# Down projection of an MLP on one Trainium2 core: three of four quarters token-major with seven block products, weight sums on GpSimd

## The reference

```python
u = rms_norm(h, norm_mlp_g[l])
h = h + jnp.square(jax.nn.relu(u @ w_mlp1[l])) @ w_mlp2[l]
```

## Time and profile before

| what | us |
| --- | --- |
| median of 3 runs | 1350.39 |
| lowest and highest run | 1349.81, 1351.56 |
| span of the profiled execution, first to last instruction | 1348.7 |
| median less that span, what lies around it | 1.7 |
| TensorE busy in that span | 1334.4 |
| VectorE, ScalarE, GpSimd busy | 939.1, 586.7, 70.7 |

### The profile page before, as it was taken

The page is one execution under the profiler, slowest core; times in us unless marked ns, Lnnn a source line. Parts: engine busy times, 40 slices in busy tenths (PEclk is TensorE's granted clock), DMA queues, the critical chain, the costliest instruction groups (busy, mean ns, idle before and its releaser), DMA issues.

```text
span 1348.7 us, 17627 instructions
## 1 busy us (share of the span) xinstructions
PE 1334.4 (99%) x6397; PEld 1094.9 (81%) x6397; DVE 939.1 (70%) x1503; ACT 586.7 (43%) x990; POOL 70.7 (5%) x60
## 2 busy tenths in 40 slices
PE   7999999999999999999999999999999999999998
PEld 6787777788888888888888888888888888888886
DVE  7868888885576543355445563599889988995685
ACT  7535655564555432114333344734333433333234
POOL 1000000102002000000013300000000000000000
PEclk9999999999999999999999999999999999999999
DMA  5333333243323333323333342323233223323332
GB/s 164 94 93 79 73 74 89 63 141 97 107 80 107 95 93 110 93 76 112 94 93 93 94 121 83 97 78 93 73 98 95 82 76 89 87 74 109 98 106 94
DMA packets 224104, 127.02 MB, mean 94 GB/s; under 512 B 21234, under 2 KB 214851, under 8 KB 224034
## 3 DMA queue, kind: packets, MB, share of 16 engines
q1 hardware_dynamic: 222418, 123.47, 31.9%
q10 hardware_dynamic: 1616, 2.62, 0.6%
HBM read 123.98 MB, written 2.10 MB: 93 GB/s over the span
## 4 chain that ended last, share of the span: by engine, by line
PE 97%; DVE 2%; ACT 1%; issue 0%; ACTq 0%; DVEq 0%
PE lin L668 26%; PE lin L671 26%; PE lin L672 26%; PE ob L1095 1%; PE sc L760 1%; PE sc L1051 1%; PE sc L1054 1%; PE sc L1055 1%; PE tr L773 1%; PE ob L797 1%; PE sc L784 1%; PE tr L1054 1%; PE lin L1054 1%; PE tr L1055 1%; PE lin L1055 1%; PE tr L1051 1%
## 5 line engine op out<-in xcount | busy, mean ns | idle before, releaser
L1719 DVE TENSOR_TENSOR wl<-raw,wh 128x1024 fp32r<-128x1024 f32 (+2 forms) x235 | 287.2, 1230 | 62.1 <-ACT wh L1228 57.7
L1228 ACT ACTIVATE wh<-raw 128x1024 fp32r<-128x1024 f32 (+2 forms) x235 | 238.8, 1022 | 134.9 <-DMA raw<-in_w_mlp_dram 44.2
L668 PE MATMUL lin<-uh,wh 128*128 128x512 f32 x624 | 249.8, 400 | 0.5 <-DVE ul L1791 0.4
L672 PE MATMUL lin<-uh,wl 128*128 128x512 f32 x624 | 243.2, 390 | 0.0
L671 PE MATMUL lin<-ul,wh 128*128 128x512 f32 x624 | 243.1, 390 | 0.0
L668 PE MATMUL lin<-vh,wh 128*128 128x512 f32 x512 | 202.6, 396 | 0.2 <-DVE te L2369 0.2
L671 PE MATMUL lin<-vl,wh 128*128 128x512 f32 x512 | 199.6, 390 | 0.0
L672 PE MATMUL lin<-vh,wl 128*128 128x512 f32 x512 | 199.3, 389 | 0.0
L668 PEld LDWEIGHTS lin<-uh,wh 128*128 128x128 f32 x624 | 117.2, 188 | 27.8 <-issue 4.4
L671 PEld LDWEIGHTS lin<-ul,wh 128*128 128x128 f32 x624 | 117.3, 188 | 25.1 <-issue 2.2
L672 PEld LDWEIGHTS lin<-uh,wl 128*128 128x128 f32 x624 | 117.1, 188 | 24.7
(11 more groups left out here) (555 smaller groups left out, 2085.2 us busy)
## 6 DMA issues: line engine op xcount, KB each, us to landing
raw<-in_w_in_dram SPq DMA_DIRECT2D x100, 512.0 KB, 3.8
raw<-in_w_mlp_dram SPq DMA_DIRECT2D x64, 512.0 KB, 4.0
raw<-in_w_out_dram SPq DMA_DIRECT2D x16, 512.0 KB, 3.7
raw<-in_w_xkv_dram SPq DMA_DIRECT2D x8, 512.0 KB, 3.7
raw<-in_w_proj_b_dram SPq DMA_DIRECT2D x8, 512.0 KB, 3.8
raw<-in_w_proj_a_dram SPq DMA_DIRECT2D x8, 512.0 KB, 3.7
xtok<-in_x_dram ACTq DMA_DIRECT2D x4, 512.0 KB, 5.0
raw<-in_w_mla_out_dram SPq DMA_DIRECT2D x4, 512.0 KB, 3.5
```

The lines of the kernel that those rows point to most:

```text
L668: ins = pe.matmul(o, wh[:, slot, at], xh_, start=start, stop=False)
L672: return pe.matmul(o, wl[:, slot, at], xh_, start=False, stop=stop)
L1228: act.activation(wh[:, c.slot(4), 0:size], raw[:, c.slot(2), 0:size], ACT.Copy).then_inc(hi_made, 1)
L1719: dve.tensor_tensor(wl[:, c.slot(4), 0:size], raw[:, c.slot(2), 0:size], wh[:, c.slot(4), 0:size].bitcast(F32), ALU.subtract).then_inc(lo_ ...
```

## The change

**Quarters.** The hidden features are taken in four quarters of 1024. `up` of a quarter: 8 jobs as before. `down` of quarters 0 to 2 is token-major, with seven block products; `down3` is feature-major as before, 8 jobs of one chunk each.

**Seven products.** The tokens are two halves of 256, the output features two halves of 512, and the hidden tiles of a quarter are paired, even and odd (four pairs kk). VectorE makes four sums of activation blocks per pair (`sums`, 128 x 256 each), ScalarE their high parts, VectorE their low parts (`sums_low`). GpSimd makes sums of weight blocks: three dependent ones per pair while chunks 0 to 7 pass, and one per pair later, 16 adds of 128 x 512 per quarter. A quarter has 14 chunks of 12 matmuls: chunks 2kk and 2kk+1 carry four products of a pair into the banks X, Q, P and R, chunks 8 to 13 carry three. Each product is 2 token blocks x 3 parts per pair.

**Loads.** A quarter has 12 loads through three raw slots (`raw2` is new): for r under 8 the whole even tile (512 KB) and the right half of the odd tile (256 KB) in turns, then the four odd tiles whole. Load r waits for the slot of r - 3, that is for the low part of that chunk, and for some of them a sum.

**Sums of products.** VectorE adds the banks into 14 blocks of 128 x 512 in SBUF (`part`; copies in quarter 0). In `up3` it combines them in 16 adds (`combine`), TensorE turns them back to feature-major with 32 transposes in the middle of jobs (`turn_acc`), and VectorE scales them and adds them to `h` (`turned_added`).

**Order.** The loops of the MLP are written out. The norm's reciprocal is waited for inside `up0`. The bias table of VectorE stands in `down3` after job 4, GpSimd's iota and mask behind the quarters. Some semaphores between two VectorE instructions are replaced by the common `step`. `acc` of the convolution is renamed `cacc`.

The core of the diff (leading blanks cut):

```diff
@@ -66,8 +66,8 @@
 PHASES = [("latent", 6, 6), ("conv", 8, 8), ("mvalues", 1, 0), ("heads", 28, 28), ("mla_out", 4, 8), ("conv_out", 4, 8),
-  ("w_out", 12, 12), ("xq", 4, 4), ("xv", 4, 0), ("xo", 4, 8), ("up0", 16, 16), ("down0", 16, 8), ("up1", 16, 16),
-  ("down1", 16, 8), ("values", 8, 0), ("av", 8, 0),
+  ("w_out", 12, 12), ("xq", 4, 4), ("xv", 4, 0), ("xo", 4, 8), ("up0", 8, 8), ("down0", 14, 0), ("up1", 8, 8),
+  ("down1", 14, 0), ("up2", 8, 8), ("down2", 14, 0), ("up3", 8, 8), ("down3", 8, 8), ("values", 8, 0), ("av", 8, 0),
...
+sh = sb("sh", [P, 4, 2, 256], F32R)
+sl = sb("sl", [P, 4, 2, 256], F32R)
+acc = sb("acc", [P, 4, 2, S])
...
+s4h = sb("s4h", [P, 4, 256], F32R, st)
+s4l = sb("s4l", [P, 4, 256], F32R, st)
+acc5 = sb("acc5", [P, 2, S], stack=st)
+raw2 = sb("raw2", [P, 1024], stack=st)
...
+RAW_SLOTS = (raw[:, 1, :], raw[:, 0, :], raw2[:])
+SLOT_LANDED = (raw_landed[1], raw_landed[0], raw2_landed)
+T2S = (vtok[:].rearrange("p q d -> p (q d)"), logit[:, 512:1024], qt[:], kt[:])
+SF = first_turned[:].rearrange("p t x -> p (t x)")[:, 0:1024].rearrange("p (n t) -> p n t", n=4)
+PART_X, PART_Q, PART_P, PART_R = (sc[0], sc[1]), (lin[0], lin[1]), (sc[2], ob), (tr[0], tr[1])
+atok_flat = atok[:].rearrange("p q d -> p (q d)")
+SUM_X1, SUM_P, SUM_X2, SUM_R2 = ((acc[:, n, 0, :], acc[:, n, 1, :]) for n in range(4))
+SUM_Q1, SUM_Q2, SUM_R1 = (acc5[:, 0, :], acc5[:, 1, :]), (nlog[:], bias[:]), (atok_flat, te[:])
+ACC_BLOCKS = ((SUM_X1, SUM_R2), (SUM_Q2, SUM_Q1))
...
+    def seven_free(u, r):
+        c = SEVEN0[u]
+        if r < 8:
+            sp.wait_ge(lo_made, c + r + 1)
+            if r == 6:
+                sp.wait_ge(sums_made, seven_sum(u, 3, 3))
+        else:
+            sp.wait_ge(lo_made, c + r + 1 + (r > 9))
+            sp.wait_ge(sums_made, seven_sum(u, r - 8, 4))
+    for q in range(4):
+        c, _ = phase(f"up{q}")
+        for m in range(DT):
+            if q and m < 2:
+                seven_free(q - 1, 9 + m)
+            load(c + m, a["w_mlp1"][0], q * FFQ + P * m, DT, P)
+        c, _ = phase(f"down{q}")
+        rows = a["w_mlp2"][0][q * FFQ:(q + 1) * FFQ, :]
+        if q == SEVENS:
+            for m in range(DT):
+                load(c + m, rows, P * m, DT, P)
+            continue
+        for r in range(SEVEN_LOADS):
+            if r < 2:
+                sp.wait_ge(lo_made, c.static - 1 + r)
+            elif r == 2:
+                if q:
+                    seven_free(q - 1, 11)
+                else:
+                    sp.wait_ge(lo_made, c.static)
+            else:
+                seven_free(q, r - 3)
+            kk, odd = (r // 2, r % 2) if r < 8 else (r - 8, 1)
+            first, n = (512, 512) if r < 8 and odd else (0, 1024)
+            tile = 2 * kk + odd
+            sp.dma_start(RAW_SLOTS[r % 3][:, 0:n], rows[tile * P:(tile + 1) * P, first:first + n])\
+                .then_inc(SLOT_LANDED[r % 3], 16)
...
+    add_squares("mlp")
+    for u in range(SEVENS):
+        first = SEVEN0[u]
+        for kk in range(4):
+            ra, rb = 2 * kk, 2 * kk + 1
+            even, odd = RAW_SLOTS[ra % 3], RAW_SLOTS[rb % 3]
+            pool.wait_ge(SLOT_LANDED[ra % 3], seven_landed(u, ra))
+            pool.wait_ge(SLOT_LANDED[rb % 3], seven_landed(u, rb))
+            if kk:
+                pool.wait_ge(sums_made, seven_sum(u, kk - 1, 3))
+            pool.tensor_tensor(odd[:, 512:1024], even[:, 512:1024], odd[:, 0:512], ALU.add).then_inc(sums_made, 1)
+            pool.wait_ge(sums_made, seven_sum(u, kk, 1))
+            pool.tensor_tensor(even[:, 512:1024], even[:, 0:512], even[:, 512:1024], ALU.add).then_inc(sums_made, 1)
+            pool.wait_ge(sums_made, seven_sum(u, kk, 2))
+            pool.tensor_tensor(T2S[kk], even[:, 512:1024], odd[:, 0:512], ALU.add).then_inc(sums_made, 1)
+        for kk in range(4):
+            r = 8 + kk
+            pool.wait_ge(SLOT_LANDED[r % 3], seven_landed(u, r))
+            pool.wait_ge(lo_made, first + 2 * kk + 2)
+            pool.tensor_tensor(T2S[kk], T2S[kk], RAW_SLOTS[r % 3][:, 0:512], ALU.add).then_inc(sums_made, 1)
+    pool.wait_ge(std_made, NORM_NO["mlp"] + 1)
+    pool.wait_ge(lo_made, CHUNK0["up3"])
+    pool.memset(sum_h[:], 0.0).then_inc(sums_cleared, 1)
+    pool.memset(sum_x1[:], 0.0).then_inc(sums_cleared, 1)
+    pool.wait_ge(sums_cleared, 2)
+    pool.wait_ge(h_added, DT)
...
+    def seven_part(banks, left, k, weights, slot, half, first, last, signal):
+        at = slice(512 * half, 512 * half + 512)
+        high, low_ = left
+        for r in range(2):
+            tok = slice(k + r * P, k + (r + 1) * P)
+            ins = pe.matmul(banks[r][:], high[:, tok], wh[:, slot, at], start=first, stop=False)
+            if weights and r == 0:
+                ins.then_inc(chunk_entered, 1)
+            pe.matmul(banks[r][:], low_[:, tok], wh[:, slot, at], start=False, stop=False)
+            ins = pe.matmul(banks[r][:], high[:, tok], wl[:, slot, at], start=False, stop=last)
+            if signal:
+                ins.then_inc(part_ready, 1)
...
+    def seven(u):
+        c, j = phase(f"down{u}")
+        for kk in range(4):
+            even, odd = (fh[:, 2 * kk, :], fl[:, 2 * kk, :]), (fh[:, 2 * kk + 1, :], fl[:, 2 * kk + 1, :])
+            s2, s3 = ((sh[:, kk, n, :], sl[:, kk, n, :]) for n in range(2))
+            last = kk == 3
+            x, y = c + 2 * kk, c + (2 * kk + 1)
+            pe.wait_ge(f_low, 12 * u + 3 * kk + 3)
+            pe.wait_ge(lo_made, (x + 1).v())
+            if kk == 0:
+                if u:
+                    taken(u - 1, 10)
+            seven_part(PART_X, even, 0, True, x.slot(4), 0, kk == 0, last, last)
+            if kk == 0:
+                evacuated(pe, j + -2)
+                evacuated(pe, j + -1)
+            seven_part(PART_Q, even, 256, False, x.slot(4), 1, kk == 0, last, last)
+            pe.wait_ge(lo_made, (y + 1).v())
+            seven_part(PART_P, s2, 0, True, y.slot(4), 0, kk == 0, last, last)
+            if kk == 0:
+                if u:
+                    taken(u - 1, 14)
+                else:
+                    pe.wait_ge(std_made, NORM_NO["mlp"] + 1)
+            seven_part(PART_R, s3, 0, False, y.slot(4), 1, kk == 0, last, last)
+        for g in range(2):
+            for kk in (2 * g, 2 * g + 1):
+                odd, s4 = (fh[:, 2 * kk + 1, :], fl[:, 2 * kk + 1, :]), (s4h[:, kk, :], s4l[:, kk, :])
+                w = c + (8 + kk + g)
+                pe.wait_ge(lo_made, (w + 1).v())
+                if kk == 0:
+                    taken(u, 2)
+                seven_part(PART_X, odd, 0, True, w.slot(4), 0, kk == 0, kk == 3, kk == 3)
+                if kk == 0:
+                    taken(u, 4)
+                seven_part(PART_Q, s4, 0, False, w.slot(4), 1, kk == 0, kk == 3, kk == 3)
+            w = c + (10 + 3 * g)
+            pe.wait_ge(lo_made, (w + 1).v())
+            if g == 0:
+                taken(u, 8)
+            for n in range(2):
+                kk = 2 * g + n
+                odd = fh[:, 2 * kk + 1, :], fl[:, 2 * kk + 1, :]
+                seven_part(PART_R, odd, 256, n == 0, w.slot(4), n, kk == 0, kk == 3, kk == 3)
...
+    def turn_acc(f):
+        if f > 1:
+            pe.wait_ge(h_added, f - 1)
+        for q in range(QT):
+            block = ACC_BLOCKS[f // 4][q // 2]
+            ins = pe.transpose(tr[f % 2][:, q * P:(q + 1) * P], block[q % 2][:, (f % 4) * P:(f % 4 + 1) * P],
+                               ident[:])
+        ins.then_inc(part_ready, 1)
+    for q in range(4):
+        c, j = phase(f"up{q}")
+        for m in range(DT):
+            if q and m < 2:
+                taken(q - 1, 11 + m)
+            if q == SEVENS and m in (1, 5):
+                taken(SEVENS - 1, SEVEN_PARTS + (8 if m == 1 else 16))
+            job(c + m, j + m, DT, uh, ul, before=tiles_of(u_low, U0["mlp"]) if q == 0 and m == 0 else None,
+                between={4: lambda f=m - 1: turn_acc(f)} if q == SEVENS and m else {})
+            if q == 0 and m == 3:
+                sum_total("mlp")
+        if q < SEVENS:
+            seven(q)
+    c, j = phase("down3")
+    for m in range(DT):
+        job(c + m, j + m, DT, fh, fl, before=tiles_of(f_low, 12 * SEVENS) if m == 0 else None,
+            between={4: lambda: turn_acc(DT - 1)} if m == 0 else {})
...
+    def seven_split(c):
+        u = sum(c.static >= first for first in SEVEN0) - 1
+        v, slot = c.static - SEVEN0[u], c.slot(4)
+        kk = v // 2
+        if v < 8 and v % 2 == 0:
+            act.wait_ge(sums_made, seven_sum(u, kk, 2))
+            wait(act, chunk_entered, (c + -2).v())
+            act.activation(wh[:, slot, :], RAW_SLOTS[v % 3], ACT.Copy).then_inc(hi_made, 1)
+        elif v < 8:
+            act.wait_ge(sums_made, seven_sum(u, kk, 3))
+            wait(act, chunk_entered, (c + -2).v())
+            act.activation(wh[:, slot, 0:512], T2S[kk], ACT.Copy)
```

(109 more changed lines are left out.)

227 lines of the change are left out of this document (91 added, 136 removed).

## The result

The changed kernel takes 1394.15 us (median of 4 runs, 1393.18 to 1395.21), beside 1350.39 us before (also of 4 runs): 1.0325 times as long, with a 95% interval of 1.031 to 1.0339. Forecast were 1392 us, 1371 to 1410, slower with 0.91. The profiled execution has a span of 1393.5 us. Its own time was 1395.2 us, the longest of the four.

What follows compares the result with a forecast made beforehand. The prediction took TensorE to bound the kernel, with chunk preparation too slow after the change. Its terms, -16.3 + 4.5 + 44.8 + 3 + 6 = +42, added to the median of 1350.4 gave 1392 us, range 1371 to 1410.

Steps and rivals of the forecast that it cites:

- 72 products less: Down quarters 0 to 2: 168 products each instead of 192, at 0.227 us, saving 16.3 us on the path.
- 32 transposes: Added on TensorE: 128 x 128 transposes at 0.14 us each, 4.5 us, taken whole.
- waits of three quarters: Down quarters 0 to 2: TensorE waits 14.9 us per quarter for prepared chunks, 44.8 in all, bounds 32 to 58.
- combining in up3: In up3 TensorE's second job waits for VectorE to add up the accumulators: 3 us, 2 to 4.
- bias table in down3: In down3 the table's twelve VectorE steps after job 4 delay freeing job 5's bank: 6 us, 1 to 9.
- up0: First up phase: the forecast sum has no term for it.
- The ring: First four chunk pairs of a down quarter: closed chain load, two adds, high part, low part, 8.2 us against 5.44 of work.
- The port: VectorE and GpSimd in down quarters: an add and a VectorE operation wait for each other, some 1.1 us per add.
- rival 1: Down quarters: port costs little because VectorE and GpSimd happen to miss each other; +31, 1381 us; chance 0.18.
- The quarter's 14.9: Waits in each of down quarters 0 to 2, before Q banks and chunks 1, 2, 4, 6 and 8: 14.9 us together.
- The rival on the other side: Down quarters: TensorE stays the bound and keeps the whole gain, 1338.6 us; chance 0.07.

Runs made afterwards that it cites:

- turned_no_sums: Changed kernel with extra landing slot, reordered queues at the up-to-down turn, bias table and waits moved, GpSimd's weight sums left out: 1341.7 us.
- no_sums: Changed kernel without GpSimd's 48 weight adds and all waits for them: 1363.5 us.
- four_slots: Changed kernel with a fourth raw landing slot, so a load may run a chunk earlier: 1388.1 us.
- fills: Changed kernel with each GpSimd weight add replaced by three write-only fills of nearly the same total length, all waits kept: 1383.1 us.
- three_edits: Changed kernel with the bias table moved to the av phase, up3's wait put right before its transposes, X banks taken before chunk 9's low part: 1382.3 us.
- turned_early: Changed kernel with extra slot, moved table and waits, reordered turn, plus chunks 0 to 2 earlier and 3 and 4 before the last up job's sums: 1371.7 us.

## Why the prediction was right

By its own steps, measured in the changed kernel:

| step | predicted | measured |
|---|---|---|
| 72 products less | -16.3 | -15.8 (43.5 to 38.3 in each of three quarters, turned_no_sums) |
| 32 transposes | +4.5 | +3.8 (0.12 each in up3, 0.5 in down3) |
| waits of three quarters | +44.8 (32 to 58) | +44.0 (14.8, 15.2, 14.0), of it 31.6 waits |
| combining in up3 | +3 (2 to 4) | +2.7 |
| bias table in down3 | +6 (1 to 9) | +9.2 |
| up0 | 0 | +0.9 |
| sum | +42 | +44.8 by spans, +43.8 by medians |

The rows for the quarters and for down3 compare lengths of phases, so they hold slow products too; what that hides stands below.

**The ring.** Predicted 8.2 us per pair, measured 7.8. It is the chain that was written down: from the end of chunk 2's low part (571.98) to the first add 2.7 (load and issue were put at 2.9), two adds to 577.29 with 2.6, high part and hops 1.1, low part 1.3. The load of 256 KB landed in 2.6 us, estimated at 2.7. That it is this chain, not VectorE or TensorE, is shown by no_sums and four_slots, which each take the waits before chunks 4 and 6 away.

**The port.** Predicted 1.1 us per add that meets a VectorE operation; the row shows 1.78 for 0.69, the same 1.1. The fills show that reading is what hurts: same waits, nearly the same duration, no slowing. The Trainium skill's rule (SBUF — State Buffer, Who interferes with whom), that a VectorE instruction with two SBUF inputs and a GpSimd read exclude each other for a whole instruction, agrees with these rows; rival 1 needed luck, and didn't get it.

**Where the total hides errors.** The quarter's 14.9 was right as a sum, but not in its parts. Predicted were 2.6 (Q banks and chunk 1), 4.8 (chunk 2), 2.7 and 2.7 (chunks 4 and 6), 2.0 (chunk 8). Down1 has 1.4, 4.4, 0, 2.3 and 2.6, 3.9 us of slow products and 0.6 in small pieces. Of the slow products, 2.3 us stand between chunk 2's gap and chunk 4: they fill the time in which TensorE would have waited for chunk 4, whose low part ends at 579.75, 2.2 us after a chunk 4 at full speed would have been due (572.12 + 5.44). So that wait would have been about what was predicted. The 1.6 us behind chunk 8's gap have no later wait to hide them and are a plain loss.

Over the three quarters the 44.0 us are 31.6 of waits (10.7, 10.7, 10.2), 10.4 of products at half speed and 2.0 in small pieces. By the same reckoning, an estimate, 8.4 of the 10.4 (2.9, 2.3 and 3.1) stand in front of a further wait and only took its place, so at full speed the waits would have been about 40 us, not 44.8. The mechanism was right, the ring above all. That the total fits to 2 us is in part luck: the start of a quarter cost less than predicted, and half speed, which was not in the sum, made up for it.

**What was mis-sized.** The bias table: 9.2 where 6 was taken, with 9 as the bound. The 6 was a choice between its bounds, not a sum. Of the 9.2, 7.2 go with the table's place (three_edits); 1.6 of the 9.2 are products at half speed behind the gap of 6.8. The other 2 stay without the table. What the sum left out shows in the rows: VectorE's round of a job was taken as its free length, but its low part takes 2.34 us in place of 1.22 with one of GpSimd's square sums inside. Its rounds are 6.5 us long (783.59 to 790.12) where TensorE's are 5.44, so VectorE falls back by 1.1 us per job and the table starts late. No run took those square sums away, so their share isn't measured by itself. A wait of 0.9 us before down0's first product stood in the sum at nothing.

**The rival on the other side** (1338.6 us, TensorE stays the bound) needed waits under 3.9 us per quarter. turned_no_sums shows that its arithmetic was right, 1341.7 with 2 us of down3 left, and that only the sums stand between: it would need adds that neither lie in the chain nor take VectorE's port.

So of the 44 us, by runs: 11 to 14 are the port (fills; 11 by the medians, 14 by the quarters), 17 to 20 the adds' time in the chain (fills to no_sums), 22 the order of the queues, the slots, the table and the combining (no_sums to turned_no_sums), 3 are left in turned_no_sums, and against them stand the 12 that products less transposes give back. The shares overlap: with a better order, taking the sums away gives 21 us instead of 31.

## What to carry to other kernels

When a change lets each loaded block feed fewer products, compute the preparation as a closed ring (load, add, high part, low part, slot free) and hold it against the new time per block, before counting the products saved: here 7.8 against 5.44 us foretold the slower kernel. It isn't the only limit, though: with the ring opened (four_slots) only 6 us came back, since the same adds then met VectorE's work at the turn. An idle engine isn't a free one: GpSimd was busy 5% of the time before, and the 62 us of adds given to it cost VectorE up to 36 us, most of it in operations with two SBUF inputs at the turn from up to down. And a saving of 16 us spread over three phases is gone with one wait of 5 us in each.

## What was not expected of the hardware

**Half speed behind a gap.** After TensorE had waited 4.27 us, the granted clock in the changed kernel was 0.50 (third column from the end of this window's row), and products started 0.43 us apart:

```profile
572.10:574.70 2.60, 2.58 (x6) 2.12 (x7) 1.08 (x2) 0.00 (x0) 0.04 (x1) 0.50 0.47 137
```

That is 1.2 GHz in place of 2.4. Eleven products ran so there, 2.3 us lost. It isn't the same each time: behind chunk 6's gap of 2.25 in down1 no product was slow, behind the one of 2.26 in down2 eight were, from the sixth on (1.6 us); behind the gaps of 1.75 us in down1 and down2 of no_sums none was, behind the 2.77 in its down0 eight were, and in turned_no_sums, without gaps, none in the quarters. So a long wait cost up to about 3 us on top of its length in these kernels (2.96 in down1 of turned_early, behind 4.96), unless the next wait hides it. A stretch's granted clock shows it at once.

**Small operations suffer most.** VectorE's sums of 256 columns take 0.42 us alone and 1.37 to 1.51 beside GpSimd's adds, over three times as long, where 1024 columns take 1.9 for 1.22: the surcharge is 0.7 to 1.1 us per operation, whatever its size. That is why the turn from up to down, with its dozen short operations, was the dearest place for the adds. Nor is it only operations with two SBUF inputs: the first two steps of the bias table have one (795.25 and 796.81 above) and took 1.52 and 1.40 us beside GpSimd's square sums, where the next two of their kind took 0.43 each.
